# A hybrid decoder layer: first loads in two-k-tile pieces, four more zero matmuls, one weight copy ahead of the copies of h, memory sums after the first hidden group

## What is computed

```python
def swiglu_ffn(x, gain, w_gate, w_up, w_down):          # D_MODEL = 1024, D_FF = 2816
    h = rms_norm(x, gain)
    return (jax.nn.silu(h @ w_gate) * (h @ w_up)) @ w_down

def reference(...):
    x = x + 0.5 * swiglu_ffn(x, ffn1_norm, ffn1_w_gate, ffn1_w_up, ffn1_w_down)
    h = rms_norm(x, mix_norm)
    ... = split(h @ w_in)      # gated DeltaNet, block-sparse attention, attention to 256 memory tokens
    y_mem = memory_attention(cq, rms_norm(mem, mem_norm), w_mem_kv, ...)
    x = x + concatenate([y_gdn, y_moba, y_mem]) @ w_out
    x = x + 0.5 * swiglu_ffn(x, ffn2_norm, ffn2_w_gate, ffn2_w_up, ffn2_w_down)
    return x
```

## Time and profile before

| | |
|---|---|
| median of 3 runs | 1122.56 us (1120.73 to 1125.46) |
| the profiled execution | 1126.8 us |
| its span, first to last instruction | 1125.0 us |
| PE busy | 1104.7 us, 98% of the span |
| DVE / ACT / POOL busy | 546.8 / 386.6 / 411.7 us |
| mean granted TensorE clock | 0.988 of full |

### The profile page before, as it was taken

One profiled execution on the slowest core, in us unless ns is written; L12 is line 12 of the kernel. 1 busy time (PEld: TensorE's weight loads), 2 busy tenths in 40 slices (PEclk: granted clock), 3 DMA queues, 4 the chain that ended last, 5 costly groups with the idle time before them and its releaser, 6 DMA issues. The chain is left out here.

```text
span 1125.0 us, 13980 instructions
## 1 busy us (share of the span) xinstructions
PE 1104.7 (98%) x5478; PEld 922.2 (82%) x5478; DVE 546.8 (49%) x757; ACT 386.6 (34%) x527; POOL 411.7 (37%) x117
## 2 busy tenths in 40 slices
PE   9999999999999999999998999999999999999998
PEld 7978888888888778789896877888888888888886
DVE  5744434344444769923425444466434334453444
ACT  7522222222222514353436555243232221323220
POOL 0264444344343314343432400252643434434340
PEclk9999999999999989999999999899999999999999
DMA  8342232322223212322010000121323222222311
GB/s 299 113 150 86 101 112 75 112 86 100 100 86 112 75 38 75 112 75 75 16 61 1 2 1 1 38 96 54 122 103 112 75 112 89 97 104 82 112 37 75
DMA packets 16019, 94.89 MB, mean 84 GB/s; under 512 B 2160, under 2 KB 2416, under 8 KB 5744
## 3 DMA queue, kind: packets, MB, share of 16 engines
q1 hardware_dynamic: 15984, 94.39, 23.4%
HBM read 92.29 MB, written 2.10 MB: 84 GB/s over the span
## 5 line engine op out<-in xcount | busy, mean ns | idle before, releaser
L349 POOL TENSOR_TENSOR wlo<-raw,whi 128x2048 fp32r<-128x2048 f32 x80 | 370.3, 4630 | 554.8 <-ACT whi L410 554.8
L1154 PE MATMUL bank<-ahi,whi 128*128 128x512 f32 x944 | 373.6, 396 | 2.6 <-POOL wlo L349 1.4
L1154 PE MATMUL bank<-alo,whi 128*128 128x512 f32 x944 | 370.8, 393 | 0.0
L1154 PE MATMUL bank<-ahi,wlo 128*128 128x512 f32 x944 | 370.7, 393 | 0.0
L410 ACT ACTIVATE whi<-raw 128x2048 fp32r<-128x2048 f32 x80 | 152.5, 1910 | 345.9 <-PE bank L1154 324.3
L1154 PEld LDWEIGHTS bank<-ahi,whi 128*128 128x128 f32 x944 | 179.5, 190 | 42.1 <-ACT ahi L432 2.6
L1154 PEld LDWEIGHTS bank<-ahi,wlo 128*128 128x128 f32 x944 | 179.4, 190 | 38.0
L1154 PEld LDWEIGHTS bank<-alo,whi 128*128 128x128 f32 x944 | 179.7, 190 | 37.0
L842 DVE SCALAR_TENSOR_TENSOR x<-bank,x 128x512 f32<-128x512 f32 x176 | 121.2, 690 | 88.1 <-PE bank L1154 87.4
L1154 PE MATMUL bank<-hhi,whi 128*128 128x512 f32 x352 | 137.2, 390 | 1.8 <-DVE x L842 1.7
L1154 PE MATMUL bank<-hhi,wlo 128*128 128x512 f32 x352 | 137.0, 389 | 0.0
(11 more groups left out here) (243 smaller groups left out, 941.5 us busy)
## 6 DMA issues: line engine op xcount, KB each, us to landing
raw<-stream SPq DMA_DIRECT2D x80, 1024.0 KB, 4.7
raw<-stream SPq DMA_DIRECT2D x6, 512.0 KB, 6.1
out<-x SPq DMA_DIRECT2D x8, 256.0 KB, 2.0
x<-x_in SPq DMA_DIRECT2D x3, 512.0 KB, 7.8
memx<-mem_in SPq DMA_DIRECT2D x2, 512.0 KB, 10.1
raw<-stream SPq DMA_DIRECT2D x3, 256.0 KB, 7.0
cst<-const_in SPq DMA_DIRECT2D x1, 704.0 KB, 6.9
x<-x_in SPq DMA_DIRECT2D x2, 256.0 KB, 4.6
```

The lines of the kernel that those rows point to most:

```text
L349: nc.gpsimd.tensor_tensor(wlo[:, u % RING, :], raw[:, u % RAW, :], whi[:, u % RING, :].bitcast(F32), ALU.subtract).then_inc(w_lo, 1)
L1154: ins = E.matmul(dst, a, b, start=(n == 0 and i == 0), stop=(n == last and i == 2))
```

## The change

Four edits. The first pieces of the weights and of x are of two k tiles throughout, four pieces in place of five, and the small vectors are loaded first. Fourteen matmuls on zeros stand where ten did. In the loop of both FFNs, ACT makes the high part of U_{i+1} (`hi(3)`) ahead of the two copies of h. The memory sums stand behind DVE's hidden part of group 0.

```diff
-PIECES = [0, 1, 2, 4, 6, 8]
+PIECES = [0, 2, 4, 6, 8]
+NP = len(PIECES) - 1
...
-            for i in range(5):
+            sp.dma_start(small[:], small_in).then_inc(small_sem, 16)
+            for i in range(NP):
                 k0, k1 = PIECES[i], PIECES[i + 1]
-                part(0, 256 * k0, 256 * k1, w0_in[i] if i < 4 else raw_in[0])
+                part(0, 256 * k0, 256 * k1, w0_in[i] if i < NP - 1 else raw_in[0])
                 sp.dma_start(x[:, k0:k1, :], x_in[:, k0:k1, :]).then_inc(x_sem[i], 16)
-                if i == 0:
-                    sp.dma_start(small[:], small_in).then_inc(small_sem, 16)
...
+                    hi(3)
                     act.wait_ge(w_used, 6 * j + (u0 + 3 * b - 1))
                     for a in range(2):
                         act.wait_ge(h_done, 4 * j + (n0 + 2 * b + a + 1))
                         A.activation(hhi[:, 2 * b + a, :], gbuf[:, a, :], ACT.Copy).then_inc(h_hi, 1)
-                    hi(3)
                     hi(4)
                     hi(5)
...
                 ffn_hidden(lambda a: n0 + a)
                 ffn_low(lambda a: n0 + a, 0)
+                if f == 0:
+                    dve.wait_ge(ab_hi, 1)
+                    V.tensor_tensor(ablo[:], abr[:], abhi[:].bitcast(F32), ALU.subtract).then_inc(ab_lo, 1)
+                    mem_sums()
                 with dve.Fori(0, FG // 2) as j:
...
             x_stat(0, 0)
-            dve.wait_ge(ab_hi, 1)
-            V.tensor_tensor(ablo[:], abr[:], abhi[:].bitcast(F32), ALU.subtract).then_inc(ab_lo, 1)
-            mem_sums()
             ffn(0)
...
-                    for _ in range(10):
+                    for _ in range(14):
                         E.matmul(psum[7][:], warm[:, 0:P], warm[:], start=True, stop=True)
```

More of the change, by code:

```diff
@@ L214, in build @@
         mem_sems = [sem(f"mem_in{i}") for i in range(2)]
-        w0_in = [sem(f"w0_in{i}") for i in range(4)]
+        w0_in = [sem(f"w0_in{i}") for i in range(NP - 1)]
         half_in = [sem(f"half_in{i}") for i in range(3)]
@@ L219, in build @@
         gain_ready, cv_raw = sem("gain_ready"), sem("cv_raw")
-        x_sem = [sem(f"x_in{i}") for i in range(5)]
+        x_sem = [sem(f"x_in{i}") for i in range(NP)]
         raw_in = [sem(f"raw_in{i}") for i in range(RAW)]
@@ L435, in x_square @@
                 A.activation(x_sq[stage][:, d, :], x[:, d, :], ACT.Square).then_inc(sq_ready, 1)
-            for i in range(5):
+            for i in range(NP):
                 k0, k1 = PIECES[i], PIECES[i + 1]
-                if i < 4:
+                if i < NP - 1:
                     part_hi(0, 256 * k0, 256 * k1, w0_in[i], 16, piece_hi)
@@ L736, in x_stat @@
                     mem_low(4, 8)
-                    part_lo(2, 0, 1024, piece_hi, 6, piece_lo)
+                    part_lo(2, 0, 1024, piece_hi, NP + 1, piece_lo)
                     part_lo(2, 1024, 2048, w_hi, 3, w_lo)
@@ L745, in x_stat @@
                 if stage == 0:
-                    part_lo(3, 0, 1024, piece_hi, 7, piece_lo)
+                    part_lo(3, 0, 1024, piece_hi, NP + 2, piece_lo)
                     part_lo(3, 1024, 2048, w_hi, 4, w_lo)
@@ L774, in _ @@
                     x_low(0, S_G1, d)
-            part_lo(1, 0, 1024, piece_hi, 5, piece_lo)
+            part_lo(1, 0, 1024, piece_hi, NP, piece_lo)
             part_lo(1, 1024, 2048, w_hi, 2, w_lo)
@@ L1195, in mem_keys @@
                     if k == 0:
-                        pe.wait_ge(piece_lo, 6)
+                        pe.wait_ge(piece_lo, NP + 1)
                     if k == 2:
@@ L1213, in mem_values @@
                     if k == 0:
-                        pe.wait_ge(piece_lo, 7)
+                        pe.wait_ge(piece_lo, NP + 2)
                     if k == 4:
@@ L1268, in first_pair @@
                         pe.wait_ge(a_hi, k + 1)
-                        if k in PIECES[:4]:
+                        if k in PIECES[:NP - 1]:
                             pe.wait_ge(piece_lo, PIECES.index(k) + 1)
-                        if k == PIECES[4]:
+                        if k == PIECES[NP - 1]:
                             pe.wait_ge(w_lo, 1)
@@ L1274, in first_pair @@
                     elif k == 0:
-                        pe.wait_ge(piece_lo, 5)
+                        pe.wait_ge(piece_lo, NP)
                     elif k == 4:
```

## The result

The changed kernel takes 1212.94 us, median of 4 runs (1212.41 to 1214.26), against 1122.75 us beside it. The ratio is 1.0803, 95% interval 1.0779 to 1.0828, which is 90.2 us slower. The forecast was 1213.

A forecast was written before the change was run, and what follows sets the result against it. PE, busy 98% of the span, was taken as the bound. Terms 61.0 (stalls) + 30.6 (clock) - 1.45 (first pass) + 0 + 0 = +90.2 on 1122.6 gave 1212.8, called 1213 us; range 1177 to 1243.

The forecast's parts named there:

- The stall: At each loop down unit's fifth tile, PE waits 3.39 us because POOL's split holds DVE's low part; 18 times, 61.0 us.
- The carried-over step: L836, never meeting POOL in the earlier trace, is held by POOL's split as L827 and L784 were.
- not held: Rival: L836 passes beside POOL or POOL waits, so the loops have no stall; 1118 to 1124 us, chance 0.07.
- the sign: In the changed profile, DVE's group of L836 has a mean near 2.9 us in place of 0.69.
- The clock: TensorE's clock falls after most loop stalls, costing 1.7 us per stall, 30.6 us over 18; bounds 0 and 61 us.
- Costs half its length: Pricing step: a stretch of PE at granted clock 0.50 costs half its length, 1.7 us for the short one.
- clock stays up: Rival: L836 is held but the clock stays up, or nearly; 1182 us, up to 1190 with a few falls, chance 0.16.
- double: Rival: L836 is held and the low-clock stretches behind the stalls are twice as long; 1243 us, chance 0.11.
- The idle of 2.21 us: PE's idle ahead of 599.57 in the earlier trace, which cost no clock; cited for the clock staying up.
- First pass: In group 0, POOL begins earlier and PE's 1.45 us wait for U_1's low part goes: -1.45 us.
- one hold over both splits: In the first pass, POOL holds the low part of h_0 up to 60.4, covered by G_1 and U_1.
- The start: New first pieces and zeros: first real matmul between 8.1 and 10.0; cost 0, between 2.6 us earlier and 3.3 later.

The follow-up runs named there:

- run 3: The changed kernel with one wait added: POOL's split of each up unit begins only when DVE's low part of h is done; 1123.26 us against 1121.99, ratio 1.001.
- Run 4: The changed kernel with 12 extra matmuls of 128x512 ahead of the fifth tile of each down unit in the loops; 1194.45 us against 1121.99, ratio 1.0645.
- loop_only: The kernel before with one edit alone: in the loops the high part of the up unit stands ahead of both copies of h; 1207.03 us against 1121.99, ratio 1.0771.
- sums_only: The kernel before with one edit alone: the memory sums stand behind the hidden part of group 0; 1122.37 us against 1121.74, ratio 0.9997.
- no_loop: The changed kernel with the old order of the loop put back; 1124.87 us against 1121.99, ratio 1.0029.
- run 9: The changed kernel with POOL's split of each loop up unit as two instructions of 1024 columns, not one of 2048; 1212.68 us against 1122.25, ratio 1.0802.
- hi_between: The changed kernel with the weight copy between the two copies of h in the loops, not ahead of both; 1199.44 us against 1122.25, ratio 1.0685.

## Why the prediction was right, point by point

**The stall: right in place, cause, count and size.** 3.39 us was forecast, 3.36 came (8.80 against 5.44), 18 times. The carried-over step, that L836 would be held like L827, was the one on which everything hung, and run 3 shows it from the other side: same order on ACT, POOL kept away, no stall. By the rule of the Trainium skill ("SBUF — State Buffer", "SBUF: two separate sides") the forecast was 3.39 too; the trace agrees, with 1.15 us from POOL's end to the end of DVE's pair in the changed kernel as in the earlier trace rows. The rival *not held* is out. L836's mean is 2.66 us, where about 2.9 was named as the sign.

**The clock: right in kind, a little too dear.** One short half-speed stretch per stall was forecast at 1.7 us, 30.6 in all. Run 4 puts the clock's own part at 27.2 us, 1.5 per stall. "Costs half its length" was the step that was a little off: matmuls start 0.43 us apart at half speed and 0.227 at full, so a low stretch costs 0.47 of its length. In the second FFN part of it also falls into PE's idle. The restart behind each wait, 2.8 us in all, was not in the sum and makes up for it: stalls and clock together were forecast at 91.6 us, and the loops became 91.3 longer. The rivals *clock stays up* and *double* are out, since the clock fell at all 18 stalls and only the first low stretch was about twice as long. The idle of 2.21 us that had left the clock alone was no guide here, but one idle of 3.21 us, the first in `loop_only`, left it alone too.

**First pass: the wait at U_1 went, as forecast, and another came.** PE no longer waits for POOL there, but 1.45 us for DVE's L824, the gate tiles of group 1, ahead of D_0. In DVE's timeline they come behind the sums, the last of which POOL held:

```profile
62.39 1.21 DVE L782 TENSOR_TENSOR memsq<-memsq 128x1024 f32<-128x1024 f32 x1
63.63 0.69 DVE L783 TENSOR_TENSOR memsq<-memsq 128x512 f32<-128x512 f32 x1
64.36 4.72 DVE L784 TENSOR_TENSOR msum<-memsq 128x256 f32<-128x256 f32 x1
69.01 1.28 DVE L824 TENSOR_TENSOR gbuf<-bank,rbc 128x512 f32<-128x512 f32 x2
```

The forecast had the gate tiles over at 65.4; they are over at 70.29. It let one hold over both splits, up to 60.4, cover both low parts of h_0. In fact each split held one of them, up to 62.33 (rows in the last section), and the third sum then met a third split, where the forecast took 0 for the three. So the first pass gave nothing, where -1.45 was in the sum. `loop_only`, with the sums in their old place, kept the gain, and by `sums_only` the sums are free with the old order of the loop (ratio 0.9997). Only with the weight copy ahead is the low part of h_0 late and pushes them into the splits.

**The start: mis-sized.** 0 was taken between -2.6 and +3.3; the pieces alone measured 1.0036, some 4 us (2.0 to 5.9), and the runs with all three small edits 3.3 and 1.1. The forecast started from the one execution it had, in which the first matmuls ran at half speed; `sums_only` and `loop_only`, at full speed from the start, show that this is not always so. The first real matmul came at 10.08 in the changed kernel, just outside the late end of 8.1 to 10.0: its piece of x was there at 8.34, no sooner than the second piece before (8.39), although it was issued about a microsecond earlier.

**The sum.** The loop was forecast at 61.0 + 30.6 - 1.45 = 90.2 and measured 86.5 by its ratio, in a run with 17 falls in place of 18. The three small edits were forecast at 0 and cost 1 to 4 us. In the profiled execution of the changed kernel D_0 begins 0.92 us later than before (70.34 against 69.42), where the sum had it 1.45 earlier, and the loops take 91.3 more. Between the loops it is 4.8 us shorter than the profiled execution before, although no edit stands there. That stretch, first before and then with the change:

```profile
363.18:805.06 441.88, 429.49 (x2477) 363.17 (x2476) 238.19 (x397) 190.78 (x332) 143.34 (x54) 0.97 0.14 51
...
411.26:848.35 437.09, 424.65 (x2478) 358.85 (x2476) 245.83 (x397) 190.58 (x331) 143.88 (x54) 0.98 0.15 54
```

The difference goes with the granted clock. In the profiled executions of the three kernels with one small edit each and of `no_loop`, the same stretch took 435.5 to 442.2 us. So a start and first pass that were 2.4 us too cheap were offset by chance elsewhere: that the median came out within a microsecond of the forecast is partly luck; that it came out near 90 is not.

## What to carry to other kernels

An instruction that is moved to an earlier place on one engine also starts what it releases on another: here ACT's copy cost DVE 2 us, which was covered, and POOL's split behind it 4.6, which was not. Ask of each two-source SBUF instruction on DVE what POOL is doing when it becomes ready, and let POOL wait for DVE where DVE is on the path. Splitting POOL's work did not help where DVE had as many instructions as POOL had pieces. A stall on TensorE that recurs can cost nearly half as much again in clock (27 us on 61 here), so it pays to price the two apart.

## What the runs showed of the hardware

**The port goes back and forth.** With both engines asking, neither got two instructions in a row in these traces. In the first pass of the changed kernel POOL had two splits back to back and DVE its two low parts (timelines of POOL and DVE):

```profile
56.73 5.05 POOL L349 TENSOR_TENSOR wlo<-raw,whi 128x2048 fp32r<-128x2048 f32 x1
...
52.63 4.70 DVE L836 TENSOR_TENSOR hlo<-gbuf,hhi 128x512 fp32r<-128x512 f32 x1 [0.36 <-ACT hhi L507]
...
57.24 5.09 DVE L836 TENSOR_TENSOR hlo<-gbuf,hhi 128x512 fp32r<-128x512 f32 x1
```

DVE's first ends at 57.33, POOL's second split takes 5.05 in place of 4.6, and DVE's second is held to its end and is over at 62.33. The halves of run 9 show the same.

**Idle of 3.2 us took the clock down nearly every time, 2.6 us mostly, 0.5 us never.** The clock fell at all 18 stalls of the changed kernel and at 17 of 18 in `loop_only`, all with about 3.2 us of idle. In `hi_between` 13 of the 17 stalls with 2.59 us of idle had a fall, and so had the one with 5.29. At the 18 places with about 0.5 us of idle in run 4 there was none. What decides the single case, no run here shows.
